# Sparse attention on one core: values as the stationary operand, probabilities weighted before they are turned, scores three units ahead

## What is computed

```python
def one_block(args):                      # 128 query tokens
    s = einsum(qb, kc) * scale            # 31 compressed keys
    p_c = masked_softmax(s, cmp_end <= t)
    o_c = einsum(p_c, vc)
    ...
    p_s = masked_softmax(s_sel, valid)    # selected blocks (here all causal ones)
    o_s = einsum(p_s, v_g)
    ...
    p_w = masked_softmax(s_win, valid_w)  # window of 512
    o_w = einsum(p_w, vwb)
    return gb[..., 0:1] * o_c + gb[..., 1:2] * o_s + gb[..., 2:3] * o_w
```

## Time and profile before

| | |
|---|---|
| median of 3 runs | 1523.92 us (1523.88 to 1524.18) |
| the profiled execution | 1524.15 us |
| its span in the trace | 1522.3 us |
| TensorE matmuls busy | 1501.3 us (99%) |
| VectorE, ScalarE, GpSimd busy | 552.7, 609.9, 666.8 us |
| the 26 units of attention | from 143.4 to 269.7 us of the span |

### The profile page before, as it was taken

How to read it: one execution, slowest core, us unless ns; L and a number is a source line. 1 busy time by engine, 2 the same in 40 slices (tenths; PEclk the granted TensorE clock), 3 DMA queues, 4 the chain that set the end, 5 groups by cost and what they waited for, 6 DMA issues and landing times.

```text
span 1522.3 us, 21544 instructions
## 1 busy us (share of the span) xinstructions
PE 1501.3 (99%) x7906; PEld 1267.7 (83%) x7906; DVE 552.7 (36%) x918; ACT 609.9 (40%) x1222; POOL 666.8 (44%) x530
## 2 busy tenths in 40 slices
PE   8999999999999999999999999999999999999998
PEld 7889999888898888888888867788888888888886
DVE  2753555454382101110006288845544111011014
ACT  4355554344443333332233468634533333333221
POOL 5542122532455445444464544453243544454442
PEclk9999999999999999999999999999999999999999
DMA  9331112331234333333232532333133332333222
GB/s 250 89 100 49 33 39 81 111 97 56 90 96 147 91 103 97 96 91 103 97 121 78 161 90 64 109 112 104 49 97 98 97 97 89 103 96 97 97 97 90
DMA packets 115714, 147.05 MB, mean 97 GB/s; under 512 B 20534, under 2 KB 74160, under 8 KB 115632
## 3 DMA queue, kind: packets, MB, share of 16 engines
q1 hardware_dynamic: 115312, 145.87, 31.3%
q0 software_dynamic: 320, 0.08, 0.0%
HBM read 143.80 MB, written 2.10 MB: 96 GB/s over the span
## 4 chain that ended last, share of the span: by engine, by line
PE 91%; DVE 4%; ACT 3%; issue 1%; POOL 1%; DMA 0%; SPq 0%; DVEq 0%; ACTq 0%
PE ps L649 81%; PE ps L881 3%; PE ps L654 2%; PE ps L861 2%; PE ps L845 1%; POOL w_lo L612 1%; DVE y_lo L1450 1%; DVE h L1742 1%; DVE h L1716 1%; PE ps L806 1%; DMA x_res<-in_x 0%; PE ps L938 0%; ACT w_hi L1082 0%; PE ps L837 0%; DVE h L1749 0%
## 5 line engine op out<-in xcount | busy, mean ns | idle before, releaser
L612 POOL TENSOR_TENSOR w_lo<-w_raw,w_hi 128x512 fp32r<-128x512 f32 (+2 forms) x468 | 601.2, 1294 | 826.7 <-ACT w_hi L1082 824.6
L1082 ACT ACTIVATE w_hi<-w_raw 128x512 fp32r<-128x512 f32 (+2 forms) x468 | 279.7, 612 | 540.0 <-PE ps L649 522.0
L649 PE MATMUL ps<-fm_hi,w_hi 128*128 128x512 f32 (+1 forms) x1112 | 422.6, 380 | 3.5 <-POOL w_lo L612 3.4
L649 PE MATMUL ps<-fm_lo,w_hi 128*128 128x512 f32 (+1 forms) x1112 | 419.7, 377 | 0.0
L649 PE MATMUL ps<-fm_hi,w_lo 128*128 128x512 f32 (+1 forms) x1112 | 419.6, 377 | 0.0
L649 PEld LDWEIGHTS ps<-fm_hi,w_hi 128*128 128x128 f32 x1112 | 209.6, 188 | 45.2 <-POOL w_lo L612 5.4
L649 PEld LDWEIGHTS ps<-fm_hi,w_lo 128*128 128x128 f32 x1112 | 209.5, 188 | 38.9
L649 PEld LDWEIGHTS ps<-fm_lo,w_hi 128*128 128x128 f32 x1112 | 209.7, 189 | 38.2 <-issue 0.5
L1877 DVE TENSOR_TENSOR gf<-silu,ps 128x512 f32<-128x512 f32 x44 | 28.3, 684 | 414.8 <-ACT silu L1417 397.6
L1624 DVE SCALAR_TENSOR_TENSOR x_res<-x_res,ps 128x512 f32<-128x512 f32 x48 | 31.4, 684 | 272.5 <-PE ps L649 187.2
L649 PE MATMUL ps<-w_hi,g_hi 128*128 128x512 f32 x288 | 112.0, 389 | 0.0
(11 more groups left out here) (280 smaller groups left out, 2219.0 us busy)
## 6 DMA issues: line engine op xcount, KB each, us to landing
w_raw<-in_f_w_up SPq DMA_DIRECT2D x352, 128.0 KB, 2.1
w_raw<-in_f_w_down SPq DMA_DIRECT2D x88, 256.0 KB, 2.6
w_raw<-in_x_wkv SPq DMA_DIRECT2D x48, 256.0 KB, 3.1
w_raw<-in_o_w_in SPq DMA_DIRECT2D x40, 256.0 KB, 2.6
w_raw<-in_x_wq SPq DMA_DIRECT2D x32, 256.0 KB, 2.7
w_raw<-in_x_wo SPq DMA_DIRECT2D x32, 256.0 KB, 2.9
w_raw<-in_e_w_in SPq DMA_DIRECT2D x24, 256.0 KB, 3.3
w_raw<-in_o_w_out SPq DMA_DIRECT2D x20, 256.0 KB, 2.6
```

Of the source, the lines that this page charges most:

```text
L612: nc.gpsimd.tensor_tensor(lo[:, :n], w_raw[:, c % RING, :n], hi[:, :n].bitcast(F32), ALU.subtract).then_inc(w_split, 1)
L649: last = nc.tensor.matmul(outp, lhsT, rhs, start=(clear and k == 0 and n == 0), stop=(k == steps - 1 and n == 2), skip_group_check=True)
L1082: nc.scalar.activation(w_pair(c)[0][:, :n], w_raw[:, s, :n], ACT.Copy).then_inc(w_rounded, 1)
```

## The change

The stationary operand of `weigh` is now the values (128 keys by 64 columns), and the turned probabilities move past it. For heads r0 and r0 + 1 the results go to output partitions 0 to 63 and 64 to 127 of the same columns of bank 6; with four heads of a group in a unit, one instruction takes two heads (256 columns), else one (128 columns). The result is already channel by channel, as the projection needs it, so `o_tok`, `o_tmp`, `turn_output` and the group `to` of the plan are gone. All units of a query block add up in bank 6 (`start` in the `cmp` unit only); one copy per query block (`output_hi`, `output_low`) takes it out. Since the weights belong to tokens, which now lie along the columns, they are put on the probabilities before these are turned (`weigh_probs`). `scores` runs three units ahead instead of two. The filling chunks are spread over 25 units and the last unit has none. Bank halves alternate by a group's place in the plan, so those of `eout0`, `eout1` and all later groups are swapped.

```diff
 def filled_until(u):
-    return max(0, u + 1) * (D // FILL * KT) // len(UNITS)
+    return min(max(0, u + 1), len(UNITS) - 1) * (D // FILL * KT) // (len(UNITS) - 1)
...
             def weigh(u):
                 qb, b, h0, heads = UNITS[u]
                 pe.wait_ge(copied_d, u + 1)
                 pe.wait_ge(copied_a, u + 1)
-                if u:
-                    pe.wait_ge(o_evac, u)
...
-                        last = nc.tensor.matmul(ps[:, 6, r * HD:(r + 1) * HD], p, v, start=(i == mine[0][0]),
-                                                stop=(i == mine[-1][0]))
+                if b == "cmp" and qb:
+                    pe.wait_ge(o_hi_ready, qb)
+                    pe.wait_ge(o_ready, qb)
+                keys = unit_keys(u)
+                per_group = min(heads, GROUP)
+                for kb in range(keys):
+                    for r0 in range(0, heads, per_group):
+                        g, pair = (h0 + r0) // GROUP, (h0 + r0) // 2
+                        for odd in (0, 1):
+                            i0 = (r0 + odd) * keys + kb
+                            half, cols = slice(odd * HD, (odd + 1) * HD), slice(pair * P, (pair + per_group // 2) * P)
...
+                            last = nc.tensor.matmul(quarter(ps[half, 6, cols]), v, p, start=(b == "cmp" and r0 == 0),
+                                                    stop=(b == "win" and kb == keys - 1), skip_group_check=True)
...
             scores(0)
             scores(1)
             evacuated("k0_1")
+            pe.wait_ge(exped, 1)
+            scores(2)
             for u in range(len(UNITS)):
                 turn_probs(u)
-                if u + 2 < len(UNITS):
-                    scores(u + 2)
+                if u + 3 < len(UNITS):
+                    pe.wait_ge(exped, u + 2)
+                    scores(u + 3)
                 for i in range(filled_until(u - 1), filled_until(u)):
                     memory_values(i)
-                for t in {len(UNITS) - 2: (0, 1), len(UNITS) - 1: (2,)}.get(u, ()):
-                    turn_output(t)
                 weigh(u)
...
+            def output_hi(qb):
+                act.wait_ge(pv_done, last_unit(qb) + 1)
+                nc.scalar.activation(fm_hi[:, 4:8, qb * P:(qb + 1) * P], quarter(ps[:, 6, :]), ACT.Copy).then_inc(o_hi_ready, 1)
...
                 if u + 2 < len(UNITS):
-                    act.wait_ge(summed, u + 1)
                     exps(u + 2)
...
+            def weigh_probs(u):
+                qb, b, h0, heads = UNITS[u]
+                dve.wait_ge(exped, u + 1)
...
+                        for r in mine:
+                            p = probs_of(u, r)
+                            last = nc.vector.tensor_scalar(p, p, weight[:, u % 2, r:r + 1], None, ALU.mult)
+                    last.then_inc(weighted, 1)
...
+            for u in range(len(UNITS)):
+                turned_half(u)
+                if UNITS[u][1] == "cmp" and u:
+                    output_low(UNITS[u][0] - 1)
+                if u + 1 < len(UNITS):
+                    weigh_probs(u + 1)
+                if u + 3 < len(UNITS):
+                    row_max(u + 3)
+            output_low(TT - 1)
```

More of the change, by code:

```diff
@@ L121, in plan_groups @@
     g += [(f"fv_{n}", KT, 1, 0) for n in range(D // FILL)]
[L122 removed]
+    g += [("attn", 0, 0, 0)]
     g += [("eout0", KT, 0, 4), ("eout1", KT, 0, 4)]
@@ L187, in filled_until, with unit_keys, last_unit @@
 def filled_until(u):
-    return max(0, u + 1) * (D // FILL * KT) // len(UNITS)
+    return min(max(0, u + 1), len(UNITS) - 1) * (D // FILL * KT) // (len(UNITS) - 1)
 def unit_blocks(u):
     qb, b, _, heads = UNITS[u]
-    return [(kb, r) for kb in range(1 if b == "cmp" else qb + 1) for r in range(heads)]
-assert all(4 < len(unit_blocks(u)) <= 8 for u in range(len(UNITS)))
+    return [(r, kb) for r in range(heads) for kb in range(unit_keys(u))]
+def unit_keys(u):
+    return 1 if UNITS[u][1] == "cmp" else UNITS[u][0] + 1
+def last_unit(qb):
+    return sum(q <= qb for q, _, _, _ in UNITS) - 1
+assert all(len(unit_blocks(u)) in (6, 8) for u in range(len(UNITS)))
 def hybrid_trunk(nc, a, out):
@@ L895, in memory_values @@
                 last.then_inc(w_used, 1)
-            def turn_output(t):
-                pe.wait_ge(o_ready, sum(b != "cmp" and qb <= t for qb, b, _, _ in UNITS))
-                for k in range(4):
-                    last = turn(ps[:, 4 * (INDEX["to"] % 2) + t, k * P:(k + 1) * P], o_tok[:, t, k * P:(k + 1) * P])
-                return last
             scores(0)
@@ L1194, in _ @@
             for u in range(len(UNITS)):
+                if UNITS[u][1] == "cmp" and u:
+                    output_hi(UNITS[u][0] - 1)
                 turned_copy(u)
@@ L1615, in _ @@
-            for t in range(TT):
-                dve.wait_ge(evac_a, ACT_BEFORE["to"] + t + 1)
-                low_part(fm_lo[:, 4:8, t * P:(t + 1) * P], quarter(bank("to", t)), fm_hi[:, 4:8, t * P:(t + 1) * P], evac_d)
+                for j in (0, 1):
+                    mine = range(j * heads // 2, (j + 1) * heads // 2)
+                    if b == "cmp":
+                        p = probs[:, u % 2, 32 * mine[0]:32 * (mine[-1] + 1)].rearrange("p (r n) -> p r n", n=32)[:, :, 0:NCMP]
+                        w = weight[:, u % 2, mine[0]:mine[-1] + 1].unsqueeze(2).to_broadcast([P, heads // 2, NCMP])
+                        last = nc.vector.tensor_tensor(p, p, w, ALU.mult)
+                    else:
+                        for r in mine:
+                            p = probs_of(u, r)
+                            last = nc.vector.tensor_scalar(p, p, weight[:, u % 2, r:r + 1], None, ALU.mult)
+                    last.then_inc(weighted, 1)
@@ L1619, in add_residual @@
+            row_max(0)
+            row_max(1)
+            weigh_probs(0)
+            row_max(2)
+            for u in range(len(UNITS)):
+                turned_half(u)
+                if UNITS[u][1] == "cmp" and u:
+                    output_low(UNITS[u][0] - 1)
[4 more added lines that the diff above has]
+            output_low(TT - 1)
             def add_residual(n, name, t):
```

85 lines of the change are left out of this document (30 added, 55 removed).

## The result

The changed kernel takes 1509.05 us (median of 4 runs, 1507.51 to 1510.17), the kernel before 1524.03 beside it (4 runs). The ratio is 0.9896, with a 95% interval of 0.9883 to 0.9910. On the 1523.92 us of before that is 1508.1 us, 0.4 under the low end of the range (1508.5). Two further sets of runs of the changed kernel have medians of 1507.91 and 1507.97 (beside 1524.37 and 1524.06 of before); experiments are compared with these two. The profiled execution took 1507.51 us against 1524.15, 16.6 less, where the prediction had summed 10.2.

A forecast was written before the change was run, and what follows sets the result against it. TensorE was taken as the bound: 8.5 us in the units + 1.76 output transposes + 0.76 wait - 0.85 new wait = 10.2 off 1524.15, giving 1514.0, and 1513.8 us against the median; range 1508.5 to 1521.

The forecast's parts named there:

- What bounds the kernel: Whole kernel: TensorE, busy 1501.3 of 1522.3 us; what is taken off its own work comes off the end.
- Two output halves run at once: Attention product: matmuls into partitions 0 to 63 and 64 to 127 overlap; failure costs 6.2 us, 1530, chance 0.15.
- The number of slots, n/2 + 1: Attention product: 9 slots for 16 matmuls, 7 for 12, 5 for 8 of 256 columns.
- its better bound: Attention units: end slots overlap the change of shape (4.1 us), which costs 0.31 (1.0 us): 1508.7 us.
- The length of a slot: Attention product: a pair of matmuls takes 0.115 us with 128 columns, 0.225 us with 256.
- The change of shape: TensorE around each attention product: in and out of the new shape together cost 0.35 us per unit.
- the `cmp` units: Products of the 4 `cmp` units: 1.48 us for 1.92 + 0.20, together 2.6 us saved.
- Output and last unit: End of attention: 16 transposes save 1.76 us, the wait before `eout0` 0.76; a new last-unit wait costs 0.85.
- VectorE: Weighting in attention: costs nothing; a `qb` 3 unit needs 3.3 us against TensorE's 4.17, leaving 0.9 of room.
- the rival on VectorE: Attention: weighting at 0.69 us plus GpSimd's 0.74 makes VectorE the bound, 6.2 us over 16 units: 1520; chance 0.10.
- The range: Whole kernel: 1508.5 to 1521 us, holding the forecast and VectorE's case, 0.8 together, without the two slow rivals.
- the worse side: Attention product: if a pair takes a fifth more than forecast, 5.2 us less is won: 1519 us.

The follow-up runs named there:

- the run on one half: Changed kernel with all products written to partitions 0 to 63, both heads on one half: 1529.34 us, ratio 1.0037 to the kernel before.
- one half after the other: Changed kernel with the loop over `odd` outermost, queueing all matmuls of one half, then all of the other: 1514.59 us, ratio 0.9920 to the kernel before.
- the run with paired products: Changed kernel with products of two neighbouring units standing together, 15 visits to the half-width shape instead of 26: 1507.57 us, ratio 0.9896 to the kernel before.

## Why the prediction was too careful, step by step

- **What bounds the kernel.** Right. The chain stays on TensorE, and the gain in its work is the gain in time.
- **Two output halves run at once.** Right, and the run on one half shows it as the cause: 21 us.
- **The number of slots, n/2 + 1.** Wrong, and the main part of the miss. The step said that the two matmuls of one instruction cannot overlap, so that the first and the last of a unit are alone. They do not overlap each other, but the other head's instruction starts 6 ns later and runs both its passes beside both of these: n/2 slots. The prediction gave its own price for this under its better bound, 16 x 0.115 + 10 x 0.225 = 4.1 us.
- **The length of a slot.** 0.109 and 0.216 us where 0.115 and 0.225 were taken. The 0.060 us for a pair of L806 was the group's 7.70 us over 128 pairs, and its 0.005 over a single one was read as a time that each pair adds. The pairs go at 0.056, the pace of one; the rest is five longer steps, 0.38 us together, and the modelled end of the last matmul. 112 x 0.006 + 40 x 0.009 = 1.0 us.
- **The change of shape.** 0.29 us a unit for 0.35, from rows of two other shapes: 26 x 0.06 = 1.6 us. In those rows the way out of the 31-column transposes was taken against 1.71 us for 16 loads; single loads there follow every 0.109 us, 1.75 in all, which makes it 0.12 for 0.16. By the product's own rows it is real and it is paid in every unit, as the Trainium skill has it (TensorEngine Tiling (Array Packing), Key Properties); more visits cost 0.29 each in the unit shown and 0.24 on average.
- These three come to 6.7 us, and the gain in the units came out 6.0 above the forecast (14.5 for 8.5). The rest is small and on the other side: the `cmp` units were credited with 0.20 for an exit that took 0.14, and the last product takes 1.09.
- **Output and last unit.** 1.75 for 1.76, 0.76 as said, and a wait of 0.77 us for 0.85: right.
- **VectorE.** Right that it costs nothing, wrong in the room. (The operation of 1.27 us in the earlier trace rows that it called a product is the addition into `o_tok`.) 3.3 us of 4.17 was forecast, 0.9 to spare; it is 3.5 of 3.94, 0.4 to 0.5. TensorE took less of the time, and GpSimd more of VectorE's. The group of weightings shows what one row of before could not (busy us, mean ns of one):

```profile
L1617 DVE TENSOR_SCALAR probs<-probs,weight 128x512 f32<-128x512 f32 x16 | 10.4, 690 | 0.3
```

- 0.69 us on average against the 0.43 of the earlier trace rows, exactly the price that the rival on VectorE had assumed. It is a mean of two kinds: ten of the sixteen took 0.48 to 0.49 us, and six took 0.96 to 1.05, each beside 0.68 us or more of GpSimd's work. The rival failed on its other part: the collisions and this price are one thing and not two to be added.
- **Not asked.** What the lead of three is worth (12 us). The prediction took it as given that what moves beside other work is free, and named the cover only for the copies.
- **The range.** It left the better bound, 1508.7, as its edge, which had the end slots and part of the change of shape (0.31) in it, and the length of a slot only on the worse side. With all three the sum is 10.2 + 6.7 = 16.9, 1507; what came is 15.9 in the stage and the 0.4 of the four transposes behind it.

## What to carry to other kernels

Where a product loads 128 columns and moves few, swap its operands, and put pairs of outputs on the two halves of the partitions: the swap alone loses here, the pair gains 21 us. Keep the work of the halves within four matmuls of each other in the queue, as far as was tried here, and count up to 0.29 us for each visit to the half-width shape. When TensorE gets faster, look at once at what runs next behind it: here some 3 us less work on TensorE brought 0.6 in the stage and nothing that runs can tell, since VectorE had 0.4 us of room per unit. And when a mechanism is already at work elsewhere in the trace, read the single starts, not only the mean of the group; the mean of 0.030 us hid that pairs have no cost of their own.

## What the runs showed of the hardware that was not expected

- As the starts read, a matmul of one output half starts ahead of three earlier ones of the other half that are still queued (one half after the other: second half from 229.453 us, the first half's last at 229.775; the same in the units of 12).
- A product that has had to wait can run out of step: the last product's starts are 0.036 and 0.073 us apart in turn (252.399, 252.435, 252.509, 252.544), each half at its own 0.109, and the product takes no longer for it (1.024 us). That it comes of the halves' blocks being copied by different engines is not shown.
- Entry and exit of the half-width shape each cost in two places, 0.09 us at the change and 0.05 at the matmul after it.
- Beside GpSimd's work on the remainders VectorE's work stretches by very different factors: the gate on 128x2 from 0.17 to 0.65 us, a weighting of 512 columns from 0.41 to 1.07 and, in the run with paired products, 1.47.
